# Two mixers of an fp32 transformer kernel: projections, ropes and compression in another order, the gate values' gelu moved beside projections

## The reference

```python
z = n @ mix_w_in[l]
zq, zkv, zg, zuv, zga, zgb = jnp.split(z, IN_SPLITS_2, axis=-1)
q = zq.reshape(B, S, NSA_HEADS, HEAD_DIM)            # 8 heads of 64
kv = zkv.reshape(B, S, 6, NSA_KV_GROUPS, HEAD_DIM)   # k_cmp, v_cmp, k_sel, v_sel, k_win, v_win
y_a = _nsa(q, kv..., gates, cmp_pe[l], cmp_w1[l], cmp_w2[l])
y_b = _gmlp(zuv, gm_ln_g[l], gm_ln_b[l], gm_ws[l], gm_bs[l])
merged = sigmoid(zga) * (y_a @ proj_a[l]) + sigmoid(zgb) * (y_b @ proj_b[l])
h = h + mod[:, 1, 2] * (merged @ w_out[l])
# _nsa: qr, ks, kw = rope(...); kc, vc = silu(blocks of 32 + pe, stride 16, @ w1) @ w2; kc = rope(kc)
#       o = g0 * softmax(q kc) vc + g1 * softmax(q ks) vs + g2 * softmax(q kw) vw
# _gmlp: u, v = split(gelu(uv)); v = layernorm(v); u * (W_s v + b) in chunks of 128
```

## Time and profile before

| | us |
|---|---|
| median of 3 runs (3456.32 to 3460.36) | 3458.29 |
| the profiled execution's own time | 3457.76 |
| its span (first to last instruction) | 3455.9 |
| PE busy | 3337.0 (97%) |
| DVE busy | 1821.0 (53%) |
| ACT busy | 1296.4 (38%) |
| first mixer: projections behind the three q's / attention passes 1 and 2 | 1542.86 to 1624.43 / to 1717.67 |
| second mixer: the same | 2686.87 to 2766.54 / to 2858.04 |

### The profile page before, as it was taken

The page is one execution under the profiler, slowest core; times in us unless marked ns, Lnnn a source line. Parts: engine busy times, 40 slices in busy tenths (PEclk is TensorE's granted clock), DMA queues, the critical chain, the costliest instruction groups (busy, mean ns, idle before and its releaser), DMA issues.

```text
span 3455.9 us, 47207 instructions
## 1 busy us (share of the span) xinstructions
PE 3337.0 (97%) x20113; PEld 2705.2 (78%) x20113; DVE 1821.0 (53%) x3062; ACT 1296.4 (38%) x2160; POOL 116.1 (3%) x210
## 2 busy tenths in 40 slices
PE   7999989999999999998899999999999989999998
PEld 5878756888888888887568888888888756788887
DVE  5565664577666665654754533353334475453333
ACT  4232565335434422233543422232223355342222
POOL 0000000010000011100000000000000000000000
PEclk9999999999999999999899999999999999999999
DMA  3110013464444365642112222222323211222321
GB/s 139 39 50 24 31 44 110 158 221 151 154 152 153 109 237 189 241 143 89 32 55 86 98 95 94 98 92 98 98 98 123 87 46 50 81 92 97 99 96 68
DMA packets 100547, 364.11 MB, mean 105 GB/s; under 512 B 11632, under 2 KB 11696, under 8 KB 99696
## 3 DMA queue, kind: packets, MB, share of 16 engines
q1 hardware_dynamic: 75888, 272.14, 23.3%
q0 software_dynamic: 24448, 88.95, 7.8%
HBM read 358.94 MB, written 2.10 MB: 104 GB/s over the span
## 4 chain that ended last, share of the span: by engine, by line
PE 88%; DVE 7%; ACT 4%; issue 1%; DMA 0%; POOL 0%; DVEq 0%; ACTq 0%; POOLq 0%
PE ps_run L435 86%; PE ps_run L796 1%; ACT nrm L1188 1%; DVE wl L1916 1%; ACT wh L1188 1%; ACT nP L1188 0%; DVE nst L2604 0%; DVE nrm L1923 0%; DVE nrm L1916 0%; DVE ug L1916 0%; DVE AL L1916 0%; DMA vec<-vec 0%; DVE dP L2285 0%; ACT ug L1188 0%; DVE HL L1923 0%
## 5 line engine op out<-in xcount | busy, mean ns | idle before, releaser
L435 PE MATMUL ps_run<-HH,wh 128*128 128x512 f32 (+1 forms) x2776 | 1068.8, 385 | 9.9 <-DVE wl L1916 3.5
L435 PE MATMUL ps_run<-HL,wh 128*128 128x512 f32 (+1 forms) x2776 | 1048.9, 378 | 0.0
L435 PE MATMUL ps_run<-HH,wl 128*128 128x512 f32 (+1 forms) x2776 | 1048.8, 378 | 0.0
L1916 DVE TENSOR_TENSOR wl<-st,wh 128x1024 fp32r<-128x1024 f32 x511 | 625.3, 1225 | 723.8 <-ACT wh L1188 723.7
L1188 ACT ACTIVATE wh<-st 128x1024 fp32r<-128x1024 f32 x511 | 538.2, 1054 | 722.8 <-PE ps_run L435 717.4
L435 PEld LDWEIGHTS ps_run<-HH,wh 128*128 128x128 f32 x2776 | 524.5, 189 | 115.2 <-issue 7.2
L435 PEld LDWEIGHTS ps_run<-HL,wh 128*128 128x128 f32 x2776 | 525.1, 189 | 97.4 <-issue 5.0
L435 PEld LDWEIGHTS ps_run<-HH,wl 128*128 128x128 f32 x2776 | 524.8, 189 | 97.4
L435 PE MATMUL ps_run<-AH,wh 128*128 128x512 f32 (+1 forms) x1167 | 445.5, 382 | 1.9 <-DVE wl L1916 1.9
L435 PE MATMUL ps_run<-AH,wl 128*128 128x512 f32 (+1 forms) x1167 | 440.7, 378 | 0.0
L435 PE MATMUL ps_run<-AL,wh 128*128 128x512 f32 (+1 forms) x1167 | 440.6, 378 | 0.0
(11 more groups left out here) (408 smaller groups left out, 3360.8 us busy)
## 6 DMA issues: line engine op xcount, KB each, us to landing
st<-wst SPq DMA_DIRECT2D x511, 512.0 KB, 3.3
mb<-ada POOLq DMA_DIRECT2D x144, 512.0 KB, 4.4
cw<-cw POOLq DMA_DIRECT2D x4, 1024.0 KB, 6.1
X<-xT SPq DMA_DIRECT2D x8, 256.0 KB, 9.1
X<-xT POOLq DMA_DIRECT2D x8, 256.0 KB, 5.6
out<-X SPq DMA_DIRECT2D x8, 256.0 KB, 2.9
kc<-kc POOLq DMA_DIRECT2D x1, 1139.5 KB, 7.2
mb<-cond POOLq DMA_DIRECT2D x2, 512.0 KB, 5.2
```

What stands on the lines that cost most here:

```text
L435: i = self.e.matmul(out, lhsT, rhs, start=start, stop=stop, skip_group_check=True)
L1916: self.e.tensor_tensor(out, a, b, op).then_inc(*self.w.done(*points))
```

## The change

It moves work of the two mixers. On TensorE the gate values come directly behind the three q's, with the ropes of q0, q1, q2 after their blocks 0, 2 and 4; each further rope comes after the first two blocks of the projection behind (q3's inside ks, ks's inside kw, kw's inside c0); the sparse values come last, with three blocks ahead of the compression and one block after each of its steps. Banks: (0,1,2) for projections and the compression, (3) for ropes, (4..7) for the wide ones. On ScalarE and VectorE the gelu of the gate values, their centring, squares, variance and root (`gate_values`) stand beside the projections q3 to c1, two steps at each; copies of Vs and the gates' sigmoids come last ahead of "heads act". Within attention only the layer norm's scaling is left, and u starts one group a step. Two of the gate-value tiles have other buffers. A slab that holds sparse values is split in its 560 columns with data alone. Cut:

```diff
@@ -311,13 +311,15 @@
...
         self.cos2, self.sin2 = self.cs2[:, 0:512], self.cs2[:, 512:1024]
-        self.ugate, self.ugate_v = ug[0:4], ug[4:6] + [self.cos2, self.sin2]
+        self.ugate = ug[0:4]
+        self.ugate_v = ug[4:6] + [self.sb(f"ugv{i}", 512, at=self.base + i * t4) for i in (2, 6)]
         self.nPT = self.tiles("nPT", 4, at=top - 12 * t4)
...
         self.cP, self.gates = [c[:, 128 * g:128 * g + 128] for g in range(2)], c[:, 256:352]
+        self.vst = [c[:, 384 + 4 * i:388 + 4 * i] for i in range(4)]
         self.cst = [[c[:, 352 + 12 * g + 4 * i:356 + 12 * g + 4 * i] for i in range(3)] for g in range(2)]
...
@@ -979,29 +985,35 @@
...
         nm = ("mix_w_in_2", (l,))
-        dense = (0, 1, 2, 3)
-        ropes = []
-
-        def lin(name, cols, ring=dense):
-            finish(self.linear((key, name), fe(cols, *nm, 8), m.HH, m.HL, None, ring))
-            self.rope((key, ropes.pop(0)), "perm64", m.nrm[0], 512, (4, 5))
+        dense, wide, turns = (0, 1, 2), (4, 5, 6, 7), (3,)
+
+        def turn(name):
+            self.rope((key, name), "perm64", m.nrm[0], 512, turns)
+
+        def lin(name, cols, before=None):
+            line = self.linear((key, name), fe(cols, *nm, 8), m.HH, m.HL, None, dense)
+            next(line)
+            if before is not None:
+                turn(before)
+            finish(line)
...
         self.three_linear([(key, ("q", i)) for i in range(3)], [fe(qcols[i], *nm, 8) for i in range(3)], m.HH, m.HL, f"m{l}", dense)
-        ropes += [("q", i) for i in range(4)] + ["ks"]
+        vw = [(*nm, c128(i * 128), np.arange(1304 + 512, 1304 + 1024)) for i in range(8)]
+        for k, _ in enumerate(self.wide((key, "gv"), vw, m.HH, m.HL, None, wide)):
+            if k in (0, 2, 4):
+                turn(("q", k // 2))
+        kv = 512
         lin(("q", 3), qcols[3])
-        kv = 512
-        for name, j in (("ks", 2), ("kw", 4)):
-            lin(name, c128(kv + j * 128))
-        for j in range(2):
-            lin(("c", j), c128(kv + j * 128), (6, 7))
+        lin("ks", c128(kv + 256), ("q", 3))
+        lin("kw", c128(kv + 512), "ks")
+        lin(("c", 0), c128(kv), "kw")
+        lin(("c", 1), c128(kv + 128))
         cols = np.concatenate([c128(kv + 3 * 128), c128(kv + 5 * 128), np.arange(1280, 1304), np.full(232, -1)])
-        v = self.wide((key, "v"), [(*nm, c128(i * 128), cols) for i in range(8)], m.HH, m.HL, None, dense, n=280)
-        for _ in range(4):
+        v = self.wide((key, "v"), [(*nm, c128(i * 128), cols) for i in range(8)], m.HH, m.HL, None, wide, n=280)
+        for _ in range(3):
             next(v)
-        self.rope((key, "kw"), "perm64", m.nrm[0], 512, (4, 5))
-        finish(v)
-        b = self.bank((key, "c1"), (4, 5))
+        b = self.bank((key, "c1"), dense)
         for j in range(2):
...
@@ -1010,20 +1022,22 @@
...
                 self.mm(b[32 * q:32 * q + 32, 0:128], x3[q][:, :, i], m.cw1[q // 2][:, 128 * i:128 * i + 128], i == 0, i == 15, *([(key, "c1")] if i == 15 and q == 3 else []))
-        b = self.bank((key, "cT"), (6,))
+        next(v)
+        b = self.bank((key, "cT"), dense)
         w.wait_ge(key, "ch")
         self.e.transpose(b[:, 0:128], m.nrm[0][:, 0:128], m.C("ident")).then_inc(*w.done((key, "cT")))
+        next(v)
         w.wait_ge(key, "hT")
         hT = [m.nrm[1][:, 32 * q:32 * q + 31] for q in range(4)]
-        b = self.bank((key, "kc"), (7,))
+        b = self.bank((key, "kc"), dense)
         for g in range(2):
...
         for g in range(2):
-            b = self.bank((key, "vc", g), (4, 5))
+            b = self.bank((key, "vc", g), dense)
             self.mm(b[0:31, 0:64], hT[2 + g], m.w2[1], True, True, (key, "vc", g))
-        self.rope((key, "kc"), "perm64", m.kcr, 31, (6,))
-        vw = [(*nm, c128(i * 128), np.arange(1304 + 512, 1304 + 1024)) for i in range(8)]
-        finish(self.wide((key, "gv"), vw, m.HH, m.HL, None, (3, 4, 5, 7)))
+        next(v)
+        self.rope((key, "kc"), "perm64", m.kcr, 31, turns)
+        finish(v)
         w.wait_ge(key, "heads act")
...
@@ -1087,13 +1101,9 @@
...
         nm = ("mix_w_in_2", (l,))
-        u = self.gmlp_u(l)
-        for _ in range(4):
-            next(u)
-            yield
-        for _ in range(6):
-            yield
-        yield from alternate(u, iter(range(7)))
+        yield from alternate(self.gmlp_u(l), iter(range(7)))
+        for _ in range(5):
+            yield
         w.wait_ge(key, "tril")
...
@@ -1725,13 +1747,22 @@
...
+        gate_values = self.gate_values(l)
         finish(self.spend(8))
-        for k in range(4):
+        for k in range(3):
             finish(self.spend(8))
+            rope_x(k)
+        finish(self.spend(8))
+        finish(self.spend(8))
+        for k in range(3, 6):
+            finish(self.spend(8))
+            next(gate_values)
+            next(gate_values)
             rope_x(k)
...
             finish(self.spend(8))
-            rope_x(4 + j)
+            next(gate_values)
+            next(gate_values)
             w.wait_ge(key, ("c", j))
...
@@ -1739,20 +1770,23 @@
...
                 self.act(x[64:128, 0:496], b[pairs_of(g), 16:512], ACT.Copy, (key, "cx raw", j, g), *([("free", (key, ("c", j)))] if g else []))
-        finish(self.spend(32))
+        finish(self.spend(8))
+        finish(gate_values)
+        finish(self.spend(8))
+        w.wait_ge(key, "c1")
+        w.wait_ge("turned", (key, "kw"))
+        self.act(m.nrm[0][:, 0:128], self.ps(key, "c1")[:, 0:128], ACT.Silu, ("free", (key, "c1")), (key, "ch"))
+        finish(self.spend(8))
+        self.rope_x((key, "kc"), (key, "kc"), m.kcr, n=31)
+        for g in range(2):
+            w.wait_ge(key, "vc", g)
+            self.act(m.vcr[g][0:31, :], self.ps(key, "vc", g)[0:31, 0:64], ACT.Copy, ("free", (key, "vc", g)))
+        finish(self.spend(8))
         for tb in range(4):
...
             self.act(m.gates.rearrange("p (h t) -> p h t", t=4)[:, :, tb], b[:, 256:280], ACT.Sigmoid, ("free", (key, "v", tb)))
-        w.wait_ge(key, "c1")
-        w.wait_ge("turned", (key, "kw"))
-        self.act(m.nrm[0][:, 0:128], self.ps(key, "c1")[:, 0:128], ACT.Silu, ("free", (key, "c1")), (key, "ch"))
-        for g in range(2):
-            w.wait_ge(key, "vc", g)
-            self.act(m.vcr[g][0:31, :], self.ps(key, "vc", g)[0:31, 0:64], ACT.Copy, ("free", (key, "vc", g)))
-        self.rope_x((key, "kc"), (key, "kc"), m.kcr, n=31)
-        finish(self.spend(32))
         self.w.stamp(key, "heads act")
...
@@ -1804,8 +1838,30 @@
...
         key = ("mixer", l)
-        yield
-        yield
+        for _ in range(4):
+            yield
+        yield from alternate(self.gmlp_u(l), iter(range(7)))
+        for i in range(9):
+            yield
+        w.wait_ge(key, "y", 3)
+        for j in range(4):
+            self.half((key, "yb", j), m.yT[j], m.AH[8 + j])
+        yield from self.merge(l, 1)
+
+    def gmlp_u(self, l):
+        m, w = self.m, self.w
+        key = ("mixer", l)
+        for i in range(4):
+            yield from self.spend(8)
+            w.wait_ge(key, "u", i)
+            self.act(m.ugate[i], self.ps(key, "u", i), ACT.Square, (key, "u gelu a", i))
+            yield
+            w.wait_ge(key, "u gelu b", i)
+            self.act(m.ugate[i], m.ugate[i], ACT.Tanh, (key, "u gelu c", i), scale=GC)
+
+    def gate_values(self, l):
+        m, w = self.m, self.w
+        key = ("mixer", l)
         for tb in range(5):
...
@@ -1814,38 +1870,13 @@
...
             yield
-        yield from alternate(self.gmlp_u(l), self.layer_norm(l))
-        for i in range(4):
-            yield
-        w.wait_ge(key, "y", 3)
-        for j in range(4):
-            self.half((key, "yb", j), m.yT[j], m.AH[8 + j])
-        yield from self.merge(l, 1)
-
-    def gmlp_u(self, l):
-        m, w = self.m, self.w
-        key = ("mixer", l)
-        for i in range(4):
-            yield from self.spend(8)
-            w.wait_ge(key, "u", i)
-            self.act(m.ugate[i], self.ps(key, "u", i), ACT.Square, (key, "u gelu a", i))
-            yield
-            w.wait_ge(key, "u gelu b", i)
-            self.act(m.ugate[i], m.ugate[i], ACT.Tanh, (key, "u gelu c", i), scale=GC)
-
-    def layer_norm(self, l):
-        m, w = self.m, self.w
-        key = ("mixer", l)
-        st = m.nrm[1][:, 160:176]
         for tb in range(4):
...
             w.own()
-            self.act(m.nrm[4], m.ugate_v[tb], ACT.Square, (key, "v squared", tb), accum_out=st[:, 8 + tb:9 + tb])
+            self.act(m.yT[0], m.ugate_v[tb], ACT.Square, (key, "v squared", tb), accum_out=m.vst[2][:, tb:tb + 1])
             yield
         w.wait_ge(key, "v var")
-        self.act(st[:, 12:16], st[:, 12:16], ACT.Sqrt, (key, "v std"))
-        yield
-        yield
+        self.act(m.vst[3], m.vst[3], ACT.Sqrt, (key, "v std"))
         yield
...
@@ -2546,29 +2579,39 @@
...
+        gate_values = self.gate_values(l)
         finish(self.spend(8))
...
```

(60 more changed lines are left out.)

47 lines of the change are left out of this document (26 added, 21 removed).

## The result

The changed kernel takes 3475.53 us (median of 4 runs, 3473.15 to 3483.74) against 3459.32 (4 runs, 3456.32 to 3463.07) for the kernel before: a ratio of 1.0053, 95% interval 1.0041 to 1.0065. It is slower by 16 us; 3430 had been forecast. The profiled execution took 3473.15 us, its span is 3471.1 us.

A forecast was written before the change was run, and what follows sets the result against it. TensorE is busy almost throughout, so only its waits or lower clock can give time. Attention gains 17.8 us a mixer, projections lose 3.5: 2 x (17.8 - 3.5) = 28.6 us off 3458.3 gives 3430, range 3404 to 3450 with (a) and (b).

The forecast's parts named there:

- 7.5 us of waits a mixer: First two attention passes: waits that stay, the second pass's present 5 us plus 2.5 us in the first.
- the merge's first product stands 1.5 steps nearer to its yb halves, Steps 12 and 13 have no projection to fill them: Attention: listed among the reasons that waits stay, with no size of its own.
- a new cost that I left out: Sign of error: a wait over 3 us ahead of the first yb product, or a wait of gate mixing.
- The gain of 17.8 us a mixer: First two attention passes: 92.4 us now, 68.5 if nothing waits, plus 7.5 of waits, less 1.4; bounds 9 and 23.
- (b): Rival: the clock falls in attention all the same, costing 9 us a mixer: 3448 us, chance 0.14.
- rope kw: Projections: TensorE wants kw's rope at 19.5, ScalarE copies it at 21.1, a wait of 1.6 us.
- compression: Projections: the compression, behind three sparse-value steps, waits 5.3 us for a chain that ends at 41.8.
- the end: End of the projections: TensorE waits for "heads act" ahead of attention, 1.9 us bare, bounds 1.4 to 3.2.
- Nothing: Narrow slabs, split in 560 of 1024 columns: no effect, since VectorE and ScalarE have room there.
- (c): Rival: the score chain sets the first passes, so moving the gelus frees nothing: slower, 3465 us, chance 0.07.
- (a): Rival: neither rope nor compression waits in the projections, 9.4 us more gained a mixer: 3411 us, chance 0.14.

The follow-up runs named there:

- e1: The changed kernel with three blank steps fewer on ScalarE and VectorE ahead of the y tiles, so a lag of one side step: 3451.2 us.
- e4: The changed kernel with the gate branch within attention in the order of the kernel before, on all three engines, lag one: 3434.51 us.
- e8: The changed kernel with u's 16 steps spread evenly up to the gate mixing, ScalarE and VectorE one side step behind: 3440.95 us.
- e2: The changed kernel with TensorE's blank steps between u and the gate mixing raised from 5 to 8: 3446.05 us.
- e7: e4 with the slabs of the sparse values split in full, as in the kernel before: 3440.72 us.
- e5: e4 without TensorE's wait for "heads act" ahead of attention: 3426.56 us.
- e9: e4 without TensorE's wait for "heads act" and with four sparse-value blocks, not three, ahead of the compression: 3421.96 us.
- e10: e9 with the whole gate branch (u, y, merge) on ScalarE and VectorE one side step sooner: 3480.95 us.

## Why the prediction was wrong

The miss is 3475.5 - 3430 = 45.5 us. By the runs: 24.3 us are the lag of y and the merge (after less e1), 16.7 us u's new place and its gelus' distance together (e1 less e4), and 4.5 us is what e4 lies above the forecast. The first two are in the attention part. All that the sum had for them was a term of 7.5 us of waits a mixer: "The second pass waits 5 us now, and I leave it that; with 2.5 us in the first". TensorE stood for 4.1 us in the first and 11.9 in the second pass of mixer 1, 16.0 in all, and the clock fell to 0.83 in the second. The two passes were to take near 75 us at 1.00 and took 97.6.

**The step that failed most: "the merge's first product stands 1.5 steps nearer to its yb halves".** I compared only where one product (the first that reads a yb half) stands against one halving, and found it right: that wait is there and is small, 0.85 us at the start of the third pass:

```profile
1719.14 0.47 PE L440 MATMUL ps_run<-AH,wh 128*128 128x512 f32 x1 [0.85 <-DVE AL L1948]
```

I did not count the same distance for the y tiles, which free the banks of the mixing, nor for the merge's copies (nrm), which free the banks of the merge. The diff shows the counts: 16 + 7 + 5 = 28 side steps ahead of the mixing on TensorE, 4 + 23 + 5 = 32 ahead of y on VectorE, against 4 + 6 + 12 + 7 = 29 and 7 + 23 = 30 before. The prediction named a wait of gate mixing, or one over 3 us ahead of the first yb product, as "a new cost that I left out". The first came, 2.70 us. The second did not; the 2.96 us stand at the merge's gate product ahead of it, which no sign named.

**"Steps 12 and 13 have no projection to fill them"** was seen, and left at the 5 us of waits that the second pass had before. Between u's last group and the mixing TensorE has only scores, turns and values there; at 1680 to 1684 it counts as busy for all 4 us and holds 0.50 of its clock. What the sum left out as well is that the gelus of u came to stand 4 side steps behind their products. e8 changes both and gives 10 of the 17 us back; e2, with more empty steps, was not slower. Which of the two costs the more stays open.

**The gain of 17.8 us a mixer** came from 92.4 - 68.5 = 23.9 us over the ideal (rival (b) has 26 for it, which that sum doesn't give), most of which I took to go with the gelus. e4 shows what they gave with the rest of attention as before: 9.6 us in the first pass, 0.4 in the second, 10.0 in all in mixer 1 and 8.6 in mixer 2, part of it the clock's. The gelus stood ahead of the score chain in the first pass; the second pass's waits stand at and around the gate mixing and stay. So the bound of 9 was nearer than the value.

**Projections**: forecast 84.1 us, measured 76.74 and 76.75, a gain of 4.8 and 2.9 where 3.5 lost was said. Term by term: TensorE's work 72.3 (measured 72.08 busy, right); rope kw 1.6 (0.52); compression 5.3 (2.21); clock behind it 2.5 (none: the stage holds 1.00, which was in part luck, since e4 loses 1.5 us behind the same wait); the end 1.9 (1.93, right, though 3.0 - 1.2 is 1.8); clock 0.5 (not in this stage; behind the wait, from 1620 to 1624, it is 0.68). The waits were placed right and the largest was oversized by 3.1 us. The missing term was the one set at "Nothing": narrow slabs. Two of them lie in the walked chain, and take 0.66 on ScalarE and 0.74 on VectorE where I used 1.07 and 1.23. Timelines of VectorE and of ScalarE:

```profile
1587.73 0.74 DVE L1948 TENSOR_TENSOR wl<-st,wh 128x560 fp32r<-128x560 f32 x1 [1.83 <-ACT wh L1209]
```

```profile
1587.04 0.66 ACT L1209 ACTIVATE wh<-st 128x560 fp32r<-128x560 f32 x1
```

Two such pairs are 2 x (0.41 + 0.49) = 1.8 us, and e7, with full slabs, waits 1.7 us longer. The other 1.3 us of the 3.1, and the 1.1 by which the rope's wait was oversized, are error of the walk, inside the bounds given.

**The rivals.** (c) gave 3465 for a slower kernel, from the score chain. It isn't the cause, though it had the direction: e4 keeps the moved gelus and gains 23 us over before. (b), the clock: 0.96 in pass 1 where it was 0.74, so little of it there (e5 shows what the wait ahead of attention costs in e4); in pass 2 the clock falls to 0.83, and returns to 1.00 in e4 with u and y back in their places, so here it came and went with the waits. (a) came nearest on the projections: 7.4 of its 9.4 us a mixer (84.1 - 76.7), though both waits are there in part.

**The Trainium skill**, "ScalarE: Activation LUTs", section "What ACT_TABLE_LOAD costs", has a drain beside each load; as an estimate from its figures that is 1.4 us more at the end of the projections. This case doesn't agree: the load ahead of "heads act", in ScalarE's timeline, again takes 1.28 us, the activation behind it starts 0.02 us later, and TensorE waited 1.93 us where 1.9 was worked out without the drain:

```profile
1616.74 1.28 ACT L1209 ACT_TABLE_LOAD   x1
1618.04 0.21 ACT L1209 ACTIVATE cmp<-ps_run 128x24 f32<-128x24 f32 x1
```

## What to carry to other kernels

Where engines with fixed orders are woven step by step, write down for every ring of banks at which step the producer fills and the consumer frees it, for each stage that is moved and not only for its first product. Here one side step was the best of those tried. For u, y and merge shifted together on e9, none costs 59 us and two cost 16; for y and merge alone, three instead of one cost 5 on e9 and 8 on before, and four 24 in the changed kernel. Moving work under cover paid only in the stretch where its queue was waited for; leave the order of the other stretches alone, or check its distances anew. A split whose size changes is a term of any queue chain that it lies in, even if its engine has room.

## What was not expected of the hardware

Short waits have no fixed price in clock. Two waits of 1.93 us were worth 8 us once removed (e5), the clock behind each included. A wait of 2.21 us ahead of the compression cost no clock in the changed kernel, whose stage stays at 1.00, and 1.5 us of it in e4, where code and waits of the stage are the same. The 3.7 us wait of before was followed by a window at 0.50. From these rows it can't be told when a short wait brings the clock down with it. In e10 one side step in the order of two engines, with no instruction added, cost 1.7% of the whole program.
